# One attention section, re-ordered: a slab's product, a write-back, the pieces of a delta rule and some bias rows change places

## The reference, cut to what matters

```
sh1, sc1, g1, sh2, sc2, g2 = split(silu(c) @ ada_w + ada_b, 6)
zq, zk, zv, zqkv, zg, zb, za = split(modulate(rms_norm(x), sh1, sc1) @ w_in)
# (A) attention: 8 heads of 64; latent rows add a relative bias inside a window, context keys join the softmax
p = softmax(concat([q @ k_loc + bias, q @ k_ctx]));  o_na = p @ v
# (B) gated delta rule, 4 heads of 128, chunks of 64, forwards and backwards, state from a cache
t_inv = inverse(I + strict_lower((k * beta) @ k.T * decay))
v_new = t_inv @ (v * beta) - (t_inv @ (k * beta * exp(gc))) @ s
o_g   = (q * exp(gc)) @ s + lower(q @ k.T * decay) @ v_new
s     = s * g_last + k_dec.T @ v_new
x = x + g1 * (concat([o_na, rms_norm(o_g) * silu(zg)]) @ w_out)
x = x + g2 * experts(modulate(rms_norm(x), sh2, sc2))   # top-1 group, top-2 experts of 16
```

## Time and profile before

| | |
|---|---|
| time of the profiled execution | 1278.42 us (its span 1276.6 us, 1.8 us lie around it) |
| median of the three runs | 1277.66 us |
| busy share of the span | PE 90%, PEld 44%, DVE 44%, ACT 23%, POOL 7% |
| mean granted TensorE clock | 0.956 |
| attention stretch, layer 0, 217.2 to 229.2 us | PE busy 8.46 of 12.00 us, granted clock 0.50 |
| attention stretch, layer 0, 229.2 to 243.0 us | PE busy 7.78 of 13.80 us, granted clock 0.99 |
| attention stretch, layer 0, 250.0 to 311.0 us | PE busy 55.42 of 61.00 us, granted clock 1.00 |
| attention stretch, layer 1, 858.0 to 868.0 us | PE busy 7.85 of 10.00 us, granted clock 0.53 |
| end of attention, layer 1, 923.0 to 939.0 us | PE busy 9.83 of 16.00 us, granted clock 0.79 |

### The profile page before, as it was taken

The page is one execution under the profiler, slowest core; times in us unless marked ns, Lnnn a source line. Parts: engine busy times, 40 slices in busy tenths (PEclk is TensorE's granted clock), DMA queues, the critical chain, the costliest instruction groups (busy, mean ns, idle before and its releaser), DMA issues.

```text
span 1276.6 us, 19293 instructions
## 1 busy us (share of the span) xinstructions
PE 1151.1 (90%) x7919; PEld 561.0 (44%) x7919; DVE 566.4 (44%) x1436; ACT 295.1 (23%) x725; POOL 87.0 (7%) x98
## 2 busy tenths in 40 slices
PE   4899998698999999997789999969889899999876
PEld 1465544375565333322245555436645633333222
DVE  1266885466256212121162688936734731121114
ACT  1248322223121100100022662132312211001000
POOL 0020000210001000000021100011000100000001
PEclk9899998899998999999889999979989899999998
DMA  8560134767955899999974112266575589999996
GB/s 357 180 188 1 67 104 164 233 243 292 414 179 205 314 415 414 403 429 427 420 286 131 43 66 91 82 196 222 191 321 195 203 307 395 425 392 429 428 426 231
DMA packets 83180, 335.44 MB, mean 263 GB/s; under 512 B 34303, under 2 KB 36743, under 8 KB 64647
## 3 DMA queue, kind: packets, MB, share of 16 engines
q1 hardware_dynamic: 76167, 310.66, 63.2%
q0 software_dynamic: 6912, 23.40, 5.1%
HBM read 315.43 MB, written 18.61 MB: 262 GB/s over the span
## 4 chain that ended last, share of the span: by engine, by line
PE 75%; DMA 14%; DVE 5%; issue 2%; ACT 2%; SPq 2%; DVEq 0%; ACTq 0%
PE bank L539 70%; DMA arena<-in_moe_w_dram 9%; PE bank L542 4%; DMA ring<-in_w_in_dram 2%; ACT arena L1437 2%; DMA ring<-in_ada_w_dram 2%; DVE x L1759 1%; DMA ring<-in_w_out_dram 1%; DVE arena L1751 1%; DMA inv_dram<-ring 1%; DVE x L1751 1%; SPq L1279 1%; DVE small L2073 1%; DVE ring L1759 0%; DVE small L1759 0%
## 5 line engine op out<-in xcount | busy, mean ns | idle before, releaser
L539 PE MATMUL bank<-ring,arena 128*32 128x512 f32 (+1 forms) x2560 | 403.2, 590 | 26.2 <-issue 16.8
L539 PE MATMUL bank<-arena 128*32 128x512 f32 (+3 forms) x1696 | 318.6, 564 | 21.2 <-issue 8.4
L1437 ACT ACTIVATE arena<-bank 128x512 f32<-128x512 f32 (+3 forms) x308 | 132.3, 475 | 608.2 <-PE bank L542 419.1
L539 PE MATMUL bank<-ring,hT 128*128 128x512 f32 x576 | 256.0, 601 | 4.4 <-DMA ring<-in_w_in_dram 2.8
L539 PEld LDWEIGHTS bank<-ring,arena 128*32 128x32 f32 (+1 forms) x2560 | 119.8, 114 | 224.7 <-issue 224.4
L539 PEld LDWEIGHTS bank<-ring,hT 128*128 128x128 f32 x576 | 109.3, 193 | 134.1 <-issue 129.8
L539 PEld LDWEIGHTS bank<-arena 128*32 128x32 f32 (+2 forms) x1696 | 93.8, 123 | 112.5 <-issue 89.6
L1751 DVE TENSOR_TENSOR arena<-bank,mrow 128x512 f32<-128x512 f32 x40 | 27.7, 691 | 248.2 <-PE bank L539 248.2
L539 PE MATMUL bank<-hT,ring 128*128 128x384 f32 x384 | 128.2, 488 | 0.1
L542 PE MATMUL bank<-const,arena 128*128 128x128 f32 x459 | 68.4, 286 | 26.8 <-DVE arena L1751 17.1
L539 PEld LDWEIGHTS bank<-hT,ring 128*128 128x128 f32 x384 | 71.2, 190 | 46.9 <-issue 1.3
(11 more groups left out here) (153 smaller groups left out, 862.0 us busy)
## 6 DMA issues: line engine op xcount, KB each, us to landing
ring<-in_moe_w_dram SPq DMA_DIRECT2D x62, 2048.0 KB, 15.0
arena<-in_moe_w_dram SPq DMA_DIRECT2D x34, 2048.0 KB, 14.9
ring<-in_ada_w_dram SPq DMA_DIRECT2D x24, 2048.0 KB, 8.7
ring<-in_w_in_dram SPq DMA_DIRECT2D x14, 2048.0 KB, 9.7
expert_dram<-arena SPq DMA_DIRECT2D x18, 512.0 KB, 14.5
ring<-in_w_out_dram SPq DMA_DIRECT2D x4, 2048.0 KB, 8.4
arena<-in_na_rpb_dram SPq DMA_DIRECT2D x32, 96.0 KB, 5.7
tok_dram<-arena POOLq DMA_DIRECT2D x6, 512.0 KB, 3.4
```

What stands on the lines that cost most here:

```text
L539: return nc.tensor.matmul(out, lhsT, rhs, start=start, stop=stop)
L1437: return nc.scalar.activation(out, in_, func, **kw)
```

## The change

Seven edits, all in or at the edge of the attention stretch, the same in both layers:

- PE issues the product of the first slab right behind the first scores, in place of place 2 (layer 0) or 3 (layer 1).
- The delta rule starts one place sooner (`RULE_AT = 3`), and its piece 1 is cut in two: the 24 products into the second bank and their DVE copies are a piece of their own. From `halves_first` on, each piece stands at the place it had.
- SP issues the four writes and eight reads of `blocks_back` ahead of the second slab; the two loads of the state come behind that slab.
- The second half of the bias rows is issued by POOL, ahead of POOL's six reads, with the two waits that SP had.
- ACT copies a finished tile out (`attended`) ahead of the next exponentials, not behind them.
- DVE gates the two latent tiles behind the last place, the second of them behind the first half of the output projection.
- PE turns these two tiles behind the first and the second product of the output projection; ACT copies them behind the gate rows.

SP's loads of expert weights into two of the buffers wait for the second tile's turn, as they did; that turn stands further back in PE's list.

```
-RULE_AT = 4
+RULE_AT = 3
     for i, s in enumerate(slabs):                       # mixing_plan
-        products[point].append(s)
+        if i:
+            products[point].append(s)
+        def bias_rows(queue, l, half):
+            for row in range(2):
+                for h in range(4):
+                    at = ((l * HEADS + 4 * half + h) * RPB_H + 5 - row) * RPB_W + NA_KW - GRID_W
+                    src = bass.AP(na_rpb.tensor, at, [[1, GRID_W], [RPB_W, BIAS_ROWS], [1, GRID_W]])
+                    queue.dma_start(bias[half][row * GRID_W:(row + 1) * GRID_W, h], src).then_inc(bias_in[half], 16)
...
                     last.then_inc(for_dve, 1)           # PE, end of pairs_last
+                def pairs_turned():
                     b = dve_bank("xt5", l)
                     for m in range(MATS):
...
                 elif k == 2:                            # PE; later pieces count one higher
+                    pairs_turned()
+                elif k == 3:
                     halves_first()
...
-                elif k == 13:
-                    for t in (1, 2):
-                        mixed_cols(og_ready, 3 * l + t + 1, flat(o_acc[t]), "og", l, t)
                 scores(0)
+                ada_product(mixing[0])
...
                 wout(0, 0)
+                mixed_cols(og_ready, 3 * l + 2, flat(o_acc[1]), "og", l, 1)
                 wout(0, 1)
+                mixed_cols(og_ready, 3 * l + 3, flat(o_acc[2]), "og", l, 2)
...
                 for i, name in enumerate(PRE[l]):       # SP
+                    if i == first_mixing + 1:
+                        blocks_back()
...
-                    if i == len(PRE[l]) - N_OUT + 1 - len([a for a in PRE[l][EARLY if l == 0 else 0:] if a[0] == "ada"]):
-                        blocks_back()
-                        sp.wait_ge(act_emptied, job["qkT", l, 1, 2])
-                        sp.wait_ge(kv_stored, 32 * (l + 1))
-                        bias_rows(1)
+                    if i == first_mixing + 1:
+                        state_rows()
...
                     probs_T(step)                       # ACT
+                    if STEPS[step][1] == 0 and STEPS[step][0]:
+                        attended(STEPS[step][0] - 1)
                     if step + 1 < N_STEPS:
                         probs(step + 1)
                     rule(2 * step - RULE_AT)
-                    if STEPS[step][1] == 0 and STEPS[step][0]:
-                        attended(STEPS[step][0] - 1)
...
                 attended(TILES - 1)
                 gate_rows(l, 1)
+                for t in (1, 2):
+                    mixed_T("og", t, 4)
...
                 point(POINTS - 1)                       # DVE
+                dve.wait_ge(osq_ready, 3 * l + 3)
+                inverse_root(flat(orr[:, 1:3, :]), flat(oss[:, 1:3, :]), 1.0 / GD)
+                gated(1)
...
                 out_half(0, 0)
+                gated(2)
                 out_half(0, 1)
...
+                pool.wait_ge(act_emptied, job["qkT", l, 1, 2])
+                pool.wait_ge(kv_stored, 32 * (l + 1))
+                bias_rows(pool, l, 1)
                 pool.wait_ge(gexp_ready, l + 1)
                 pool.wait_ge(solved_out, 64 * (l + 1))
```

More of the change, by code:

```diff
@@ L591, in _ @@
             for l in range(DEPTH):
-                plan = mixing_plan([name for name in PRE[l][EARLY if l == 0 else 0:] if name[0] == "ada"])
+                mixing = [name for name in PRE[l][EARLY if l == 0 else 0:] if name[0] == "ada"]
+                plan = mixing_plan(mixing)
                 def point(p):
@@ L934, in rule @@
                     elif k == 2:
+                        pairs_turned()
+                    elif k == 3:
                         halves_first()
-                    elif k == 3:
+                    elif k == 4:
                         halves_last()
-                    elif k == 4:
+                    elif k == 5:
                         new_values(0)
-                    elif k == 5:
+                    elif k == 6:
                         keys_values(0)
@@ L947, in rule @@
                         keys_state(1)
-                    elif k == 6:
+                    elif k == 7:
                         new_values(1)
                         queries_state(1)
-                    elif k == 7:
+                    elif k == 8:
                         keys_values(1)
                         weighed_values(1)
-                    elif k == 8:
+                    elif k == 9:
                         keys_state(2)
-                    elif k == 9:
+                    elif k == 10:
                         new_values(2)
@@ L1272, in _ @@
             for l in range(DEPTH):
[L1273 to L1279, removed]
                 def blocks_out():
@@ L1318, in load_slab @@
                     sp.dma_start(dst, src).then_inc(slab_in[pre_slot[name]] if done is None else done, 16)
+                first_mixing = [i for i, name in enumerate(PRE[l]) if name[0] == "ada" and i >= N_WIN][0]
                 for i, name in enumerate(PRE[l]):
+                    if i == first_mixing + 1:
+                        blocks_back()
                     if l and i < len(AHEAD):
@@ L1336, in _ @@
                     if name == ("win", l, 5):
-                        bias_rows(0)
+                        bias_rows(sp, l, 0)
                         if l == 0:
@@ L1621, in rule @@
                 def rule(k):
-                    if k == 5:
+                    if k == 6:
                         b = filled("o_ctx", l)
@@ L1635, in rule @@
                             last.then_inc(act_emptied, 1)
-                    elif k == 9:
+                    elif k == 10:
                         mixed_T("og", 0, 4)
-                    elif k == 11:
+                    elif k == 12:
                         for t in (2, 1):
@@ L1644, in rule @@
                             last.then_inc(osq_ready, 1)
-                    elif k == 13:
-                        for t in (1, 2):
-                            mixed_T("og", t, 4)
                 probs(0)
@@ L2182, in rule @@
                             last.then_inc(dve_emptied, 1)
-                    elif k == 10:
+                    elif k == 11:
                         for d in range(2):
```

15 lines of the change are left out of this document (6 added, 9 removed).

## The result

The changed kernel takes 1270.73 us (median of 15 runs, 1262.12 to 1282.79); the kernel before, run beside it, 1278.45 (1274.99 to 1287.04). The ratio is 0.992, with a 95% interval of 0.9902 to 0.9939. The direction was right and the size was not: about 8 to 10 us came (7.7 by the medians, 10.2 by the ratio) instead of 21.7, and the time lies above the range. The profiled execution has a span of 1270.0 us.

The account below looks back on a forecast made before the run. It took PE's long idles in attention (first softmax, late instructions in the pairs, late slabs, DVE's gating) as the bound. Terms -9.7 - 7.5 - 6.9 + 2.4 = -21.7 took 1278.4 to 1256.7 us; range 1251 to 1268.

Parts of the forecast that it names:

- Inputs of the pairs: Layer 0, before the first pairs: POOL's six reads issued by 222.4 and landed at 224.8, other end 232.6; hidden until 229.
- The 7.47 us: PE's stop inside layer 0's second group of pairs: instructions arriving late behind bias rows and two slabs; it would go.
- The first rival: The stall inside the pairs has another cause and stays, giving back 7.47 and 2.15 us: 1266.3 us, chance 0.20.
- First product: First slab's product right behind the first scores: 1.92 to 3.10 us into a 4.15 us idle, costing nothing.
- Third slab: Layer 0: issued at about 219, there by 233; its product starts at 236.9, not 247.17.
- Fourth slab: Layer 0: late next, there at 244.2 where PE is ready at 243.7; before 253.92. Wait under 1 us.
- Layer 0 and the start of layer 1: Attention terms: -9.7 us in layer 0 up to the fourth slab, -7.5 at the same pairs in layer 1.
- End of layer 1: Last slab's product no longer waits 4.98 us for DVE's gating and starts at 923.35, not 930.70: -6.9 us.
- turns: Eight turns of 0.145 us on PE's path in each layer's output projection: +1.2 us a layer.
- POOL and DVE: Bias issues on POOL beside DVE: could add one scaling (0.75 us) to one or two issues; sum unchanged.
- POOL's queue holding the pairs: Rival: bias rows ahead of POOL's reads delay the pairs; at 3.0 us an issue, 1286 us, slower; chance 0.06.
- the experts' stream takes the gain back: Rival: the experts' 2 MB slab stream sets their end, so an earlier start brings nothing: 1278 us, chance 0.09.

Follow-up runs that it names:

- e1: The changed kernel with POOL's bias rows issued behind its six reads of the blocks, not ahead: 1268.06 us, ratio 0.9888 to the kernel before.
- e2: The changed kernel with SP's second slab held until all 14 reads of the blocks have landed: 1264.75 us, ratio 0.9876 to the kernel before.
- e7: e1 with SP's third slab held until DVE has copied the turned pairs: 1274.92 us, ratio 0.9961 to the kernel before.
- e9: e1 with SP's second slab, and all behind it, held until DVE has copied the last pairs: 1283.19 us, one run.
- e11: The changed kernel run and profiled again, with no edit: 1270.61 us, ratio 0.9915 to the kernel before.
- e6: e4 with two waits on POOL, so its key scaling and bias mask come behind DVE's scalings: 1261.05 us, ratio 0.9853 to the kernel before.
- e10: e2 with two waits on POOL, so its key scaling and bias mask come behind DVE's scalings: 1261.37 us, ratio 0.9831 to the kernel before.
- e4: The changed kernel with all 14 reads of the blocks on SP, POOL keeping bias rows and products: 1263.22 us, ratio 0.9862 to the kernel before.
- e5: The kernel before with only the end edits (last two tiles gated and turned between output projection products): 1274.62 us, ratio 0.9949 to the kernel before.

## Why the prediction was wrong, step by step

*Inputs of the pairs: the step that failed.* POOL's issues came when forecast (the last at 222.7 for 222.4); the landing did not. (SP's eight reads started at 214.78 for 213.4; the last of them landed at 227.48, before PE came.) I had two prices, 2.4 us and 10.8, said that two slabs would be in the queues, and took the smaller, though it came from reads whose nearest slab had been issued 10 us before and had landed at 219.15, ahead of them, and the 10.8 from another kind of transfer, which I placed among slabs. The profile shows 7.7 and 10.7. The other end, 232.6, was the truth (232.82). That cost 4.37 and 4.40 us. e1 and e2 show the cause from both sides: reads ahead of the slab take 2.6 us to land, and reads with the slab held back behind them 4.0.

*The 7.47 us.* The reading, instructions that arrive late while the queues are busy, is borne out by the packets, e7 and e9; that taking the bias rows away would end it is not, and "at 233 to 236 the queues will hold hardly anything" was wrong: 415 GB/s. So the stops did not go, and 1.95 us is left in each layer. The first rival had the right mechanism in part; its prices were 7.47 and 2.15. The Trainium skill ("Runtime: NRT & Kernel Launch", section "Instruction fetch mechanics") has the cost of crossing a block "mostly hidden". In e9 the trace agrees, with no stop; with busy queues up to 7.47 us (before) and 3.64 us (e1) were not.

In the changed kernel's first profile these four gaps are 12.7 us, and the median missed by 14.0. In its second profile (e11) layer 1 lost its time to DVE's scaling instead, so the shares differ from run to run.

*First product:* right; hidden in the first idle, which is now 2.29 us. *Third slab:* wrong, and by luck without a cost. The forecast had it there by 233; it was issued at 223.90, not 219, and landed at 240.70. PE did not wait for it only because PE itself was late (245.00 instead of 236.9); e1, e6 and e10 waited 1.06, 0.79 and 1.82 us there. *Fourth slab:* 0.52 us, as forecast.

*Layer 0 and the start of layer 1 (-9.7, -7.5).* By the profile -3.7 (to the end of the stretch), and +0.3 up to the first 64 x 64 products in layer 1. In e6 and its repeat, with the reads in time and POOL's products kept away from DVE's, the two layers come near to what the terms said: 103.1 and 100.6 us (forecast 100.3) and 87.3 (88.9). With the reads alone in time they do not quite (e4: 102.6 and 90.5). So the sum was that of a kernel in which neither mishap happens.

*End of layer 1 (-6.9)* and *turns (+1.2):* right. From the first 64 x 64 products of layer 1 to the output projection the changed kernel takes 62.35 us, before 69.11: -6.8; e5 has -5.6 in the column. The turns cost 0.44 us for four (935.69 to 936.13), 0.9 a layer.

*POOL and DVE: a cost that was put at nothing.* The moved bias rows bring POOL's products forward into DVE's scalings, and a pair of scalings takes 0.76 us alone, 1.60 in the changed kernel, 4.49 in layer 1 of e11 and up to 4.87 (e2, layer 1). I cited the Trainium skill ("SBUF — State Buffer", section "SBUF: two separate sides") for DMAs that GpSimd issues. Here that cost did not show: 0.61 to 0.67 us an issue. The same section of the Trainium skill says that the pair of ports which both engines share is held by one of them for a whole instruction. The longer scalings agree with that; e6 and e10, which only keep the products apart, bring 0.76 us back. The prediction moved these products and gave them no line.

*The rivals.* POOL's queue holding the pairs was dear not by issue time but by landing. That the experts' stream takes the gain back is not borne out: e5's edits brought 6.5 us (3.5 to 9.7) where 4.5 were forecast.

## What to carry to other kernels

When a small transfer that an engine waits for is issued within some us of a large one, price its landing by rows of small transfers among large ones, and put its issue ahead of theirs. A DMA moved to another engine's list moves that engine's later work too: ask whom it then runs beside. A stop called "issue" in a run of many tiny matmuls is to be laid beside the DMA share and the packets of the instruction queue of that moment before any instruction is blamed.

## What the runs showed of the hardware that was not expected

- A 48 KB read lands in 2.6 us (median, e1), or in 7.7 (10.7 at most, changed kernel) when it is issued at the same time as a 2 MB slab.
- PE stops for instructions while the queues are busy: 19 stops of 0.29 to 7.47 us in the 120 pairs or just behind them, each ended 1.2 to 1.5 us after a 16 KB packet of the instruction queue was through; none with empty queues (e9, and layer 0 of e7).
- A pair of DVE products between two SBUF tiles took 0.76 us alone and 4.68 beside POOL's key scaling and mask (e2), while DVE's copies out of PSUM kept their 0.55 us beside the mask (e1).
- A gap can cost more than its length: in layer 0 of the changed kernel the granted clock was 1.00 from 236.7 to 239.0 us, and after the stop of 1.95 us in it 0.72 from 239 to 245; the product there took 3.25 us instead of 1.92.
